# A new order of ScalarE's and VectorE's instructions in a chunked scan and at the start of a gated MLP, in a fused kernel of three layers

## The chip, the cores and the metric

One core of one Trainium2 chip. The metric is the time of one execution on the device in microseconds (us), the median of several runs. A NeuronCore has five engines with in-order instruction streams that meet through semaphores: TensorE (PE, matmuls into PSUM), VectorE (DVE), ScalarE (ACT), GpSimd (POOL) and SyncE (SP, which here only starts DMAs).

## The reference

256 tokens of width 1024, with 16 meta tokens in front in the first block, pass through a hybrid mixer (gated causal convolution beside stick-breaking attention), a conv-gated MLP, a layer of two chunked scans, and a block-sparse attention layer. The two parts that the change touches are the MLP

```python
def conv_gated_mlp(xn, w_up_gate, conv_w_ffn, w_down):
    u, g = jnp.split(xn @ w_up_gate, 2, axis=-1)
    u = causal_dwconv(u, conv_w_ffn)               # width 3, one filter per channel
    return (jax.nn.gelu(u) * g) @ w_down           # 2816 hidden channels
```

and the scan layer, here cut to its order of work:

```python
    u = h @ w_in
    z_a, xbc, dt_raw, q_b, k_b, v_b, gate_lr, g_b = split_cols(u, EVEN_SPLITS)
    xbc = silu(causal_depthwise_conv(xbc, conv_w, conv_b))      # width 4
    y_a = ssd_chunked_scan(xs, dt, a, bm, cm, d)                # 16 heads of 64
    y_a = rms_norm(y_a * silu(z_a), ssd_norm_w)
    o_b = gla_chunked(q_b, k_b, v_b, log_decay)                 # 8 heads, chunks of 64
    o_b = rms_norm(o_b, gla_norm_w) * silu(g_b)
    out = concat([y_a, o_b]) @ w_out
```

`gla_chunked` scores each chunk's queries against its keys, carries a state from chunk to chunk (`decay * s + k^T v`), and adds what the queries read from the state. `ssd_chunked_scan` multiplies a matrix of decays with the scores of `bm` and `cm` and applies it to `dt * xs`.

## The kernel before

**Stream of weights.** All matmuls with weights are done in fp32r with weights and inputs split in a high and a low part, three matmuls for a block of 128 x 128 (high with high, high with low, low with high). `tiles_of_stream` lists the output tiles in PE's order. Almost every tile has 8 blocks, which is one chunk of 0.5 MB (the value tiles `ev` of the scan have two chunks). A chunk is loaded to `raw` by SP, its high part is written by ACT (`split_hi`, L549), the low part by DVE (`split_lo`, L1077); each of the three buffers holds 4 chunks. PE waits on `lo_ready` before it reads a chunk (`project`, L1806; L1809 for `ev`; L1834 for tiles done together). ACT may write the high part of a chunk when PE has read the chunk four before it. `feed(tile)` is this `split_hi` or `split_lo`, once for each chunk of the tile, and on both engines the calls run four chunks ahead: `feed(("eg", 2))` writes the chunk that comes four behind that of eg2, after PE has finished eg2. SP sends the DMA of a chunk when the low part of the one four before it is written.

**Order.** There is no planner: each engine's order is written out by hand in its block, with `feed` calls between the element-wise work. Where an instruction stands in an engine's order decides what waits behind it.

**Feed-forward start.** PE does fu0, fg0 and fu1 together, then fg1, fu2, fg2, fu3, fg3, fu4 and so on (fu: the conv half, fg: the gate half). For tile i DVE scales u (`ffn_up`, L1326), ACT makes the first tap (L738), DVE adds two (`ffn_conv`, L1333), ACT applies GELU (L743), POOL scales it (`ffn_scale`, L452), DVE multiplies it with PE's gate tile (`ffn_out`, L1341), and ACT and POOL split the product (L747, L458). PE may write a tile's PSUM bank when the tile that had it before has been read: fg3's bank is that of fg1, read by `ffn_out(1)`.

**The scan.** Round p (0 to 3) has the tiles eq, ek, ev of the linear attention (GLA; query, key, value of a pair of heads) and, for u = 2p and 2p+1, ez (gate of the state-space part, SSD), eg (gate of GLA) and ex (input of SSD, for u+2). Between the tiles PE does small matmuls:

- `turn_x(u)` (L2068) transposes silu(conv(x)); needs DVE's `ssd_y(u-1)` (L1464), which empties bank 5. `ssd_args(u)` (L1459) on DVE makes of it dt * x.
- `ssd_heads(u)` (L2077) needs `ssd_args(u)` and the decay matrices, which ACT makes (`decays`, L849 and L854) and POOL multiplies with the scores (`ssd_weights`, L479).
- `turn_keys(p)` (L2089) transposes the keys into bank 6, and ACT copies them (`take_keys(p)`, L870). It needs `gla_norm(p-1)` on DVE (its two reads of bank 6, L1497), which needs `gla_rms(p-1)` on ACT (L901, L903, behind a load of the activation table).
- `gla_scores(p)` (L2098) needs the copied keys and POOL's products of queries and keys with the exponentials that ACT makes in `gla_exps(p)` (13 instructions, L888 and L889). DVE masks the scores (L1479).
- `gla_kv(p)` (L2110) makes the chunks' k^T v, DVE's `gla_states(p)` (L1486, L1489) runs them through the recurrence, and `gla_out(p)` (L2120, L2123), which stands between the tiles ek and ev of the next round, needs the result.
- ACT copies ev out of PSUM in `take_values(p)` (L864).

`conv_in` (L1380) takes an ex, eb or ec tile out of PSUM, `tap` (ACT, L778) makes the first of the four taps, `conv_rest` (DVE, L1388) the other three, `z_full` (L1397) and `half_tanh` (ACT, L803) make silu of it or of a gate. `gate_y` (L1469) multiplies SSD's output with its gate, `ssd_high`/`ssd_low` and `gla_high`/`gla_low` split the results for the output projection. `decay_sums(1)` (L1413, L1417) makes the cumulated decays of rounds 2 and 3.

Of the kernel before, what the change touches and what calls it, by code (L numbers as in the profile page):

```python
# [158 lines left out]
def build(nc, xT, params, weights, masks, gate_w2, out, scratch):  # L159
    with ExitStack() as ctx:  # L160
# [362 lines left out]
        def _(act):  # L523
# [27 lines left out]
            def feed(tile):  # L551
                for _ in chunk_of(tile):
                    split_hi()
# [324 lines left out]
            def gla_exps(p):  # L878

                k = p % 2  # L880
                act.wait_ge(S("gla_bias"), p // 2 + 1)
                need(act, "gla_qk", p)
                need(act, "sc_ready", p - 1)
                need(act, "st_ready", p - 1)
                for n, (dst, scale) in enumerate(((kb[:, k, :], 1.0 / 16), (ka[:, k, :], 1.0 / 16), (em, -1.0 / 16))):
                    for c in range(4):
                        w_ = slice(64 * c, 64 * c + 64)
                        a.step(A(dst[:, w_], gcs[:, p, w_], ACT.Exp, scale=scale, bias=decay_cols[:, n, p, c:c + 1]))  # L888
                a.sig(A(eg[:, k, :], gcs[:, p, :], ACT.Exp, scale=-1.0 / 16), "gla_exp")  # L889

            def gla_squares(p):
                act.wait_ge(S("gla_o"), p + 1)
                a.sig(A(osq, bank(6), ACT.Square), "gla_sq")
# [36 lines left out]
            for p in range(1, 4):  # L930
                u = 2 * p
                feed(("ek", p))
                if p == 1:
                    gla_exps(1)
                    take_values(1)
                    feed(("ev", 1))
                    half_tanh(("ex", 3), xs[:, 3, :])
                    gla_squares(0)
                    half_tanh(("ez", 1), zs[:, 1, :])
                    act.wait_ge(S("xsilu"), 6)  # L940
                    half_tanh(("eg", 1), gs[:, 1, :])
                    ssd_high(0)
                    gla_rms(0)
                    feed(("ez", 2))
                    decays(3)
                    ssd_high(1)
                    half_tanh(("ez", 2), zs[:, 0, :])
                else:
                    gla_squares(p - 1)
                    gla_exps(p)  # L950
                    feed(("ev", p))
                    take_values(p)
                    gla_rms(p - 1)
                    feed(("ez", u))
                    half_tanh(("ez", u), zs[:, 0, :])
                    decays(u + 1)
                feed(("eg", u))
                half_tanh(("eg", u), gs[:, u % 4, :])
                gla_high(p - 1)
                if p > 1:  # L960
                    take_keys(p)
                if p < 3:
                    feed(("ex", u + 2))
                ssd_high(u)
                if p < 3:
                    tap(("ex", u + 2), u + 2, xs[:, u + 2, :])
                feed(("ez", u + 1))
                if p == 1:
                    take_keys(1)
                if p < 3:  # L970
                    half_tanh(("ex", u + 2), xs[:, u + 2, :])
                half_tanh(("ez", u + 1), zs[:, 1, :])
                if p < 3:
                    decays(u + 2)
                feed(("eg", u + 1))
                half_tanh(("eg", u + 1), gs[:, (u + 1) % 4, :])
                if p < 3:
                    feed(("ex", u + 3))
                ssd_high(u + 1)
                if p < 3:  # L980
                    tap(("ex", u + 3), u + 3, xs[:, u + 3, :])
                    feed(("eq", p + 1))
                    half_tanh(("ex", u + 3), xs[:, u + 3, :])
# [79 lines left out]
        def _(dve):  # L1063
# [279 lines left out]
            ffn_up(0)  # L1343
            ffn_up(1)
            ffn_conv(0)
            feed(("fu", 1))
            ffn_conv(1)
            ffn_out(0)
            feed(("fg", 1))
            ffn_out(1)  # L1350
# [219 lines left out]
            for p in range(1, 4):  # L1570
                u = 2 * p
                take_queries(p)
                if p == 1:
                    take_keys(1)
                    gate_both(0)
                    feed(("eq", 1))
                    conv_rest(("ex", 3), 3, xs[:, 3, :])
                    ssd_y(2)
                    feed(("ek", 1))
                    z_full(("ex", 3), xs[:, 3, :], name="xsilu")  # L1580
                    gate_both(1)
                    feed(("ev", 1))
                    z_half(("ez", 2), zs[:, 0, :])
                    ssd_args(3)
                    gla_norm(0)
                    feed(("ez", 2))
                    ssd_low(0)
                    ssd_low(1)
                else:
                    feed(("eq", p))  # L1590
                    z_full(("ex", u + 1), xs[:, u + 1, :], name="xsilu")
                    ssd_args(u)
                    take_keys(p)
                    feed(("ek", p))
                    feed(("ev", p))
                    ssd_y(u)
                    z_half(("ez", u), zs[:, 0, :])
                    gla_norm(p - 1)
                    feed(("ez", u))
                    ssd_args(u + 1)  # L1600
                z_half(("eg", u), gs[:, u % 4, :])
                feed(("eg", u))
                z_full(("ez", u), zs[:, 0, :])
                gate_y(u)
                z_full(("eg", u), gs[:, u % 4, :])
                gla_low(p - 1)
                if p < 3:
                    conv_in(("ex", u + 2))
                    feed(("ex", u + 2))
                    conv_rest(("ex", u + 2), u + 2, xs[:, u + 2, :])  # L1610
                z_half(("ez", u + 1), zs[:, 1, :])
                feed(("ez", u + 1))
                ssd_low(u)
                if p < 3:
                    z_full(("ex", u + 2), xs[:, u + 2, :], name="xsilu")
                z_half(("eg", u + 1), gs[:, (u + 1) % 4, :])
                ssd_y(u + 1)
                gla_scores(p)
                feed(("eg", u + 1))
                z_full(("ez", u + 1), zs[:, 1, :])  # L1620
                gate_y(u + 1)
                z_full(("eg", u + 1), gs[:, (u + 1) % 4, :])
                ssd_low(u + 1)
                if p == 1:
                    decay_sums(1)
                if p < 3:
                    conv_in(("ex", u + 3))
                gla_states(p)
                if p < 3:
                    feed(("ex", u + 3))  # L1630
                    conv_rest(("ex", u + 3), u + 3, xs[:, u + 3, :])
# [727 lines left out]
```

## Time and profile before

| | |
|---|---|
| median of 3 runs | 846.91 us (846.84 to 847.1) |
| the profiled execution: own time | 846.78 us |
| its span | 844.9 us |
| busy: PE, DVE, ACT, POOL | 830.4, 622.5, 504.9, 120.2 us |
| feed-forward start | 315 to 327 us of the span |
| the scan's rounds 1 to 3 | about 550 to 665 us |
| granted TensorE clock, mean over the span | 0.998 of full speed |

A view of the profile lists, for each instruction or run of equal instructions, its start in us from the span's start, its duration, engine, line, operation and operands, and in brackets how long the engine was idle before it and which instruction ended that. Matmuls are pipelined: in a steady stream they start every 0.12 us and are each shown 0.28 us long, so their starts tell the pace. The chain of waits is what ended last, followed back step by step.

### The profile page before, as it was taken

To read this page: it belongs to the slowest core of one execution; us is meant where nothing else is said; L and a number is where in the kernel's file an instruction comes from. 1 tells how busy PE (TensorE), PEld (TensorE's weight loads), DVE (VectorE), ACT (ScalarE), POOL (GpSimd) and SP (SyncE) were. 2 spreads that over 40 slices of the span, in tenths; PEclk is the share of its full clock that TensorE was granted. 3 is DMA by queue.
4 is the path that set the end of the run, shared out by engine and by line. 5 is a ranking of instruction groups with operands and counts; after the bars stand their busy time and mean duration, and the time that the engine had idled before them with its cause. 6 is when DMAs were issued, how large, how long until landed. Compare 5 with 4: busy or idle time off the path is not lost.

```text
span 844.9 us, 16864 instructions
## 1 busy us (share of the span) xinstructions
PE 830.4 (98%) x6770; PEld 799.7 (95%) x6770; DVE 622.5 (74%) x1055; ACT 504.9 (60%) x876; POOL 120.2 (14%) x119
## 2 busy tenths in 40 slices
PE   8999999999999999999999999999999999999997
PEld 7999999999999999999999999998898999888896
DVE  6647888886666688677664488999797696568765
ACT  6346657555454576555554468797868555356655
POOL 1000000000000305433441100042414010000002
PEclk9999999999999999999999999999999999999999
DMA  8744435445555536655666535545444376654431
GB/s 307 254 153 141 154 104 173 128 138 175 187 181 193 173 101 193 196 188 179 195 194 187 192 101 166 176 153 184 149 152 153 114 229 183 191 169 136 125 101 50
DMA packets 39853, 139.81 MB, mean 165 GB/s; under 512 B 4432, under 2 KB 5088, under 8 KB 39648
## 3 DMA queue, kind: packets, MB, share of 16 engines
q1 hardware_dynamic: 37728, 135.22, 50.1%
q10 hardware_dynamic: 2048, 3.51, 1.3%
q8 instruction: 54, 0.88, 0.5%
q14 instruction: 23, 0.19, 0.1%
HBM read 137.65 MB, written 1.06 MB: 164 GB/s over the span
## 4 chain that ended last, share of the span: by engine, by line
PE 82%; DVE 9%; ACT 5%; issue 1%; DMA 1%; POOL 1%; SPq 0%; DVEq 0%; ACTq 0%; POOLq 0%
PE ps L1806 66%; PE ps L1834 4%; PE ps L1809 4%; DVE weights_lo L1077 3%; ACT weights_hi L549 1%; PE ps L1949 1%; PE ps L1934 1%; DMA raw_weights<-weights_in 1%; PE ps L1963 1%; PE ps L2217 1%; PE ps L2235 1%; DVE arena L1388 1%; PE ps L2225 1%; POOL arena L479 0%; ACT arena L888 0%
## 5 line engine op out<-in xcount | busy, mean ns | idle before, releaser
L1077 DVE TENSOR_TENSOR weights_lo<-raw_weights,weights_hi 128x1024 fp32r<-128x1024 f32 x251 | 311.8, 1247 | 87.1 <-ACT weights_hi L549 86.8
L1806 PE MATMUL ps<-x_hi,weights_hi 128*128 128x256 f32 (+3 forms) x1272 | 367.8, 289 | 1.2 <-DVE weights_lo L1077 0.5
L1806 PE MATMUL ps<-x_lo,weights_hi 128*128 128x256 f32 (+3 forms) x1272 | 358.1, 282 | 0.0
L1806 PE MATMUL ps<-x_hi,weights_lo 128*128 128x256 f32 (+3 forms) x1272 | 357.9, 281 | 0.0
L549 ACT ACTIVATE weights_hi<-raw_weights 128x1024 fp32r<-128x1024 f32 x251 | 263.2, 1053 | 147.6 <-PE ps L1806 61.0
L1806 PEld LDWEIGHTS ps<-x_hi,weights_hi 128*128 128x128 f32 x1272 | 239.2, 188 | 8.7 <-issue 6.0
L1806 PEld LDWEIGHTS ps<-x_lo,weights_hi 128*128 128x128 f32 x1272 | 239.6, 188 | 0.7 <-issue 0.5
L1806 PEld LDWEIGHTS ps<-x_hi,weights_lo 128*128 128x128 f32 x1272 | 239.5, 188 | 0.0
L1806 PE MATMUL ps<-y_hi,weights_hi 128*128 128x256 f32 (+1 forms) x488 | 137.7, 282 | 0.0
L1806 PE MATMUL ps<-y_lo,weights_hi 128*128 128x256 f32 (+1 forms) x488 | 137.4, 282 | 0.0
L1806 PE MATMUL ps<-y_hi,weights_lo 128*128 128x256 f32 (+1 forms) x488 | 137.1, 281 | 0.0
L444 POOL TENSOR_TENSOR arena<-arena 128x256 f32<-128x256 f32 (+1 forms) x24 | 25.9, 1081 | 494.2 <-ACT arena L700 327.7
L1806 PEld LDWEIGHTS ps<-y_hi,weights_hi 128*128 128x128 f32 x488 | 92.0, 189 | 0.3 <-issue 0.2
L1806 PEld LDWEIGHTS ps<-y_lo,weights_hi 128*128 128x128 f32 x488 | 91.9, 188 | 0.3 <-issue 0.2
L1806 PEld LDWEIGHTS ps<-y_hi,weights_lo 128*128 128x128 f32 x488 | 92.0, 189 | 0.0
L452 POOL TENSOR_TENSOR arena<-arena,rinv 128x256 f32<-128x256 f32 x22 | 33.4, 1517 | 81.8 <-ACT arena L743 81.8
L1809 PE MATMUL ps<-weights_hi,x_hi 128*128 128x256 f32 (+1 forms) x96 | 31.0, 323 | 0.6 <-DVE arena L1380 0.6
L1809 PE MATMUL ps<-weights_lo,x_hi 128*128 128x256 f32 (+1 forms) x96 | 30.6, 319 | 0.0
L1809 PE MATMUL ps<-weights_hi,x_lo 128*128 128x256 f32 (+1 forms) x96 | 30.6, 318 | 0.0
L738 ACT ACTIVATE arena<-arena,params 128x256 f32<-128x256 f32 x22 | 11.1, 510 | 28.4 <-DVE arena L1326 28.2
L1326 DVE TENSOR_TENSOR arena<-ps,rinv 128x258 f32<-128x258 f32 x22 | 9.4, 428 | 24.9 <-PE ps L1806 24.2
L1333 DVE SCALAR_TENSOR_TENSOR arena<-arena,params 128x256 f32<-128x256 f32 x44 | 22.2, 505 | 4.2 <-ACT arena L738 1.0
(268 smaller groups left out, 1069.9 us busy)
## 6 DMA issues: line engine op xcount, KB each, us to landing
raw_weights<-weights_in SPq DMA_DIRECT2D x251, 512.0 KB, 3.8
arena<-decay_rows ACTq DMA_DIRECT2D x8, 256.0 KB, 3.9
masks<-masks_in SPq DMA_DIRECT2D x1, 1186.0 KB, 7.1
raw_weights<-weights_in SPq DMA_DIRECT2D x4, 256.0 KB, 6.0
hidden<-xT_in SPq DMA_DIRECT2D x2, 272.0 KB, 6.7
hidden<-xT_in ACTq DMA_DIRECT2D x1, 276.0 KB, 4.0
hidden<-xT_in ACTq DMA_DIRECT2D x1, 272.0 KB, 5.9
gate_w<-gate_w_in ACTq DMA_DIRECT2D x1, 256.0 KB, 3.7
```

Source lines behind the costliest of these rows:

```text
L444: ins = nc.gpsimd.tensor_tensor(sq[:, 0, t0:T], sq[:, 0, t0:T], sq[:, i, t0:T], ALU.add)
L452: g.sig(nc.gpsimd.tensor_tensor(fgl[:, i % 2, :], fgl[:, i % 2, :], rinv[:, META:T], ALU.mult), "gelu_scaled")
L549: a.sig(A(whi[:, s * CW:(s + 1) * CW], raw[:, (c % RAW) * CW:(c % RAW + 1) * CW], ACT.Copy), "hi_ready")
L738: a.sig(A(fcv[:, i % 2, :], fu[:, i % 2, 0:L], ACT.Copy, scale=pcol("conv_ffn", i)), "tap_ready")
L1077: d.sig(TT(wlo[:, s * CW:(s + 1) * CW], raw[:, (c % RAW) * CW:(c % RAW + 1) * CW], whi[:, s * CW:(s + 1) * CW].bitcast(F32), ALU.subtract) ...
L1326: d.sig(TT(fu[:, i % 2, :], r, rinv[:, TA:T], ALU.mult), "u_ready")
L1333: ins = STT(out=c_, in0=u[:, j:L + j], scalar=pcol("conv_ffn", FT * j + i), in1=c_, op0=ALU.mult, op1=ALU.add)
L1388: ins = STT(out=dst, in0=scr2[:, n % 2, j:L + j], scalar=pcol("even_conv", 10 * j + ct), in1=dst, op0=ALU.mult, op1=ALU.add)
L1806: ins = mm(bank(BANK_OF[no])[:, 0:b - a], wt, x_[:, kt, a:b], start=s0, stop=s1)
L1809: ins = mm(bank(BANK_OF[no + o])[0:t1 - t0, 0:step * P], x_[:, kt, t0:t1], wt, start=s0, stop=s1)
L1834: ins = mm(bank(BANK_OF[no])[:, 0:b - a], w_[:, at:at + P], x_[:, kt, a:b], start=kt == 0 and n == 0 and len(passes) == 2, stop=kt == KT - ...
L1934: ins = mm(bank(4 + e)[:, c0:c0 + T - t0], keysT[rows, p, k0:k0 + P], qpair[rows, p % 2, t0:T], start=n == 0, stop=n == 2, skip_group_chec ...
```

## The change

In the order of hunks:

1. ACT, rounds 2 and 3: `feed(("ev", p))` comes ahead of `gla_exps(p)`.
2. ACT, round 1: `take_keys(1)` comes right behind `feed(("eg", 2))`, ahead of the tanh of eg2; before it stood behind `feed(("ez", 3))`.
3. DVE, feed-forward start: `ffn_conv(1)` comes ahead of `feed(("fu", 1))`.
4. DVE, rounds 2 and 3: `ssd_args(u)` comes ahead of `feed(("eq", p))` and of the silu of ex.
5. DVE, round 1: `gla_states(1)` and `conv_in(("ex", 5))` come right behind `feed(("eg", 3))`; before they stood behind `decay_sums(1)`.

No instruction is added or removed; SP, POOL and PE keep their order.

```diff
--- before.py
+++ after.py
@@ -947,14 +947,16 @@
                     half_tanh(("ez", 2), zs[:, 0, :])
                 else:
                     gla_squares(p - 1)
+                    feed(("ev", p))
                     gla_exps(p)
-                    feed(("ev", p))
                     take_values(p)
                     gla_rms(p - 1)
                     feed(("ez", u))
                     half_tanh(("ez", u), zs[:, 0, :])
                     decays(u + 1)
                 feed(("eg", u))
+                if p == 1:
+                    take_keys(1)
                 half_tanh(("eg", u), gs[:, u % 4, :])
                 gla_high(p - 1)
                 if p > 1:
@@ -965,8 +967,6 @@
                 if p < 3:
                     tap(("ex", u + 2), u + 2, xs[:, u + 2, :])
                 feed(("ez", u + 1))
-                if p == 1:
-                    take_keys(1)
                 if p < 3:
                     half_tanh(("ex", u + 2), xs[:, u + 2, :])
                 half_tanh(("ez", u + 1), zs[:, 1, :])
@@ -1343,8 +1343,8 @@
             ffn_up(0)
             ffn_up(1)
             ffn_conv(0)
+            ffn_conv(1)
             feed(("fu", 1))
-            ffn_conv(1)
             ffn_out(0)
             feed(("fg", 1))
             ffn_out(1)
@@ -1587,9 +1587,9 @@
                     ssd_low(0)
                     ssd_low(1)
                 else:
+                    ssd_args(u)
                     feed(("eq", p))
                     z_full(("ex", u + 1), xs[:, u + 1, :], name="xsilu")
-                    ssd_args(u)
                     take_keys(p)
                     feed(("ek", p))
                     feed(("ev", p))
@@ -1617,15 +1617,19 @@
                 ssd_y(u + 1)
                 gla_scores(p)
                 feed(("eg", u + 1))
+                if p == 1:
+                    gla_states(1)
+                    conv_in(("ex", 5))
                 z_full(("ez", u + 1), zs[:, 1, :])
                 gate_y(u + 1)
                 z_full(("eg", u + 1), gs[:, (u + 1) % 4, :])
                 ssd_low(u + 1)
                 if p == 1:
                     decay_sums(1)
-                if p < 3:
-                    conv_in(("ex", u + 3))
-                gla_states(p)
+                else:
+                    if p < 3:
+                        conv_in(("ex", u + 3))
+                    gla_states(p)
                 if p < 3:
                     feed(("ex", u + 3))
                     conv_rest(("ex", u + 3), u + 3, xs[:, u + 3, :])
```

## Rows read from the trace of the kernel before

**Rows 1.** Timeline of TensorE, feed-forward start (start us, us, engine line op operands xcount [idle before <-releaser])

```profile
320.09 0.29 PE L1806 MATMUL ps<-x_hi,weights_hi 128*128 128x258 f32 x1
...
322.83 0.28 PE L1806 MATMUL ps<-x_hi,weights_lo 128*128 128x258 f32 x1
323.45 0.39 PE L1806 MATMUL ps<-x_hi,weights_hi 128*128 128x256 f32 x1 [0.34 <-DVE arena L1341]
...
326.86 0.36 PE L1806 MATMUL ps<-x_hi,weights_hi 128*128 128x258 f32 x1 [0.32 <-DVE weights_lo L1077]
```

**Rows 2.** Timeline of TensorE in the scan: three of its waits

```profile
581.28 1.10 PE L2098 MATMUL ps<-arena 128*128 128x256 f32 x4 [1.49 <-ACT arena L870]
...
593.21 1.05 PE L2120 MATMUL ps<-arena 128*128 128x128 f32 x7 [1.33 <-DVE arena L1489]
...
605.90 0.41 PE L2068 MATMUL ps<-masks,arena 128*128 128x128 f32 x2 [0.49 <-DVE arena L1464]
```

**Rows 3.** Timeline of ScalarE in the scan, rounds 2 and 3

```profile
597.71 2.97 ACT L888 ACTIVATE arena<-arena,decay_columns 128x64 f32<-128x64 f32 x12
...
631.56 0.42 ACT L803 ACTIVATE arena<-arena 128x256 f32<-128x256 f32 x1 [2.17 <-DVE arena L1388]
...
633.30 2.97 ACT L888 ACTIVATE arena<-arena,decay_columns 128x64 f32<-128x64 f32 x12
...
636.48 2.00 ACT L549 ACTIVATE weights_hi<-raw_weights 128x1024 fp32r<-128x1024 f32 x2
638.37 0.82 ACT L864 ACTIVATE arena<-ps,rinv_by_token 128x256 f32<-128x256 f32 x2
```

**Rows 4.** Timeline of VectorE in the scan

```profile
586.33 1.94 DVE L1077 TENSOR_TENSOR weights_lo<-raw_weights,weights_hi 128x1024 fp32r<-128x1024 f32 x1 [0.17 <-ACT weights_hi L549]
...
592.43 0.73 DVE L1489 SCALAR_TENSOR_TENSOR arena<-arena,ps 128x128 f32<-128x128 f32 x2
593.07 1.22 DVE L1077 TENSOR_TENSOR weights_lo<-raw_weights,weights_hi 128x1024 fp32r<-128x1024 f32 x1
...
606.30 0.88 DVE L1497 SCALAR_TENSOR_TENSOR arena<-ps,params,arena 128x256 f32<-128x256 f32 x2
...
612.14 1.95 DVE L1077 TENSOR_TENSOR weights_lo<-raw_weights,weights_hi 128x1024 fp32r<-128x1024 f32 x1 [1.20 <-ACT weights_hi L549]
...
628.03 0.73 DVE L1489 SCALAR_TENSOR_TENSOR arena<-arena,ps 128x128 f32<-128x128 f32 x2
```

**Rows 5.** Timeline of TensorE in the scan, rounds 2 and 3

```profile
608.98 0.38 PE L2089 MATMUL ps<-masks,arena 128*128 128x128 f32 x2
...
629.00 1.05 PE L2120 MATMUL ps<-arena 128*128 128x128 f32 x8
...
636.34 0.88 PE L2077 MATMUL ps<-arena 128*64 128x256 f32 x8
...
647.70 1.78 PE L2077 MATMUL ps<-arena 128*64 128x256 f32 x8
```

**Rows 6.** Chain of waits, 622 to 656 us (start us, us, what)

```profile
647.57 1.01 POOL arena L479
...
648.62 0.86 PE ps L2077 x4
```

**Rows 7.** Timeline of VectorE, feed-forward start

```profile
316.84 1.01 DVE L1333 SCALAR_TENSOR_TENSOR arena<-arena,params 128x256 f32<-128x256 f32 x2 [0.39 <-ACT arena L738]
318.19 1.23 DVE L1077 TENSOR_TENSOR weights_lo<-raw_weights,weights_hi 128x1024 fp32r<-128x1024 f32 x1 [0.34 <-ACT weights_hi L549]
319.52 1.29 DVE L1333 SCALAR_TENSOR_TENSOR arena<-arena,params 128x256 f32<-128x256 f32 x2
```

**Rows 8.** Timeline of GpSimd, feed-forward start

```profile
318.54 1.47 POOL L452 TENSOR_TENSOR arena<-arena,rinv 128x256 f32<-128x256 f32 x1 [21.58 <-ACT arena L743]
...
323.01 0.73 POOL L458 TENSOR_TENSOR y_lo<-arena,y_hi 128x256 fp32r<-128x256 f32 x1
```

**Rows 9.** Weight DMAs of L424 issued from 585 to 640 us

```profile
DMA to landing us min/median/max: 3.4/3.6/5.0
```

## Prediction

> **What bounds the kernel now.** I read the list of TensorE's waits first, then the timelines of all engines around each wait, then the chain of waits from 560 to 660 us. TensorE (PE) is busy nearly all the time, so a change can win only where PE waits, and lose only where it makes PE wait. It waits in the two places that the diff touches. In the feed-forward start the tile fg3 begins at 323.45 instead of 0.12 behind the matmul of 322.83, and fu4 begins at 326.86 [rows 1]. In the scan it waits 1.49 us for the turned keys of round 1 (`klt`, L870 on ScalarE), 1.33 us for the states of the same round (`gla_states(1)`, L1489 on VectorE), and about 0.5 us for `ssd_y(4)` [rows 2]. The profile's figure for a wait is too small by 0.16: at 323.45 it says 0.34, while the starts are 0.62 apart where 0.12 is the rhythm, so 0.50 is lost.
>
> These waits are one half of the picture. The other half is that ScalarE (ACT) and VectorE (DVE) pass work back and forth through every round without slack: ACT waits for the DVE's conv taps (L1388) at 631.56 [rows 3], DVE waits for ACT's `split_hi` at 612.14 [rows 4], and so on; round 2 and 3 of ACT's exponentials are 35.6 us apart (597.71, 633.30) [rows 3]. PE isn't in that loop. It is tied to it again late in round 3: `ssd_heads(7)` begins at 647.70 and takes 1.78 us [rows 5], because GpSimd (POOL) finishes its second product at 648.58 and the last four matmuls start at 648.62 [rows 6]. Whatever PE has won earlier is handed back at such a place unless the loop is shorter too.
>
> **Feed-forward start.** `ffn_conv(1)` moves ahead of `feed(("fu", 1))` on DVE. Its two instructions cost 1.01 alone, as `ffn_conv(0)` does at 316.84 [rows 7]. So they end at 317.85 + 0.07 + 1.01 = 318.93, 1.9 us earlier than now (319.52 + 1.29 = 320.81). GELU(1) on ACT and its scaling on POOL then no longer hold `ffn_out(1)`: the wait at 323.45 (0.50) goes. DVE is 0.7 earlier at `feed(("fu", 2))`, and the wait at 326.86 (0.32 + 0.16) goes too. Both first matmuls also have the next one 0.23 and 0.19 behind instead of 0.12. Together 1.1 at most.
>
> The cost is what was moved past: `feed(("fu", 1))` writes the low half of the weights of fu3 (feeds run four chunks ahead). It runs 318.19 to 319.42 now [rows 7] and PE wants it at 320.09 [rows 1]. Behind the conv it starts at 318.9, so even alone it ends at 320.1. It isn't alone. POOL asks for its scaling at 318.54: beside DVE's split that took 1.47, a like one by itself takes 0.73, and DVE's pair of 319.52 took 1.29 instead of 1.01 [rows 7, 8]. So each turn costs DVE 0.28, and two splits in a row beside POOL cost more. With 0.28 the split ends at 320.4 to 320.5, PE waits 0.4 and gets 0.1 more from the restart: net gain 1.1 - 0.5 = 0.6. With a full POOL instruction in between (0.73 and restart) it ends near 321.1 and the gain is gone (-0.1). Bounds 1.1 and -0.1; I take 0.5, since the 0.28 is the nearest row.
>
> The Trainium skill (SBUF — State Buffer, Who interferes with whom) says that GpSimd and a VectorE instruction with two SBUF inputs exclude each other, one blocking fully. The rows agree in kind. By that rule the split would wait for the whole rest of the POOL instruction, and this stage would give 0.2 instead of 0.5.
>
> **Scan, round 1.** `take_keys(1)` moves from behind `feed(("ez", 3))` to behind `feed(("eg", 2))`. There ACT idles before its next tanh, and the 0.36 us copy hides; the turned keys are long there. PE's `gla_scores(1)` starts without the wait: 1.49 + 0.16 = 1.65 [rows 2]. `gla_states(1)` and `conv_in(("ex", 5))` move ahead of four gate instructions and `decay_sums(1)` on DVE. The states end at 593.16 now [rows 4]; moved, they follow the split of 586.33, which ends at 588.27, and are done by about 589.3. `gla_out(1)` then has no wait: 1.33 + 0.16 = 1.5 [rows 2]. PE reaches the value tile ev2 about 3.2 us earlier. DVE's sum of work is the same, so `feed(("ex", 5))` still begins near 593.07 and ends near 594.29 [rows 4], and PE, which wants it now at 594.4, just isn't held.
>
> **Round 2.** `feed(("ev", 2))` goes ahead of `gla_exps(2)` on ACT. Each of its two instructions waits for PE to have read a chunk of ev2, and all of ACT's later work is queued behind. Today ev2 ends 7.34 us behind `gla_out` (629.00 to 636.34 [rows 5]), that is at 593.21 + 7.4 = 600.6; moved 3.2 earlier, at 597.4. ACT wants the second feed at 597.71 + 0.95 = 598.66, so it doesn't wait. `ssd_y(4)` comes some 3 us earlier with the feeds, and `ssd_args(4)` 1.5 earlier, which PE needs by then. But ACT's sum is unchanged, so `gla_rms(1)` ends when it did, `gla_norm(1)` still runs at 606.30 and its two reads end at 607.18 [rows 4]. PE can't turn the keys before that (bank 6): 607.2 against 608.98 now [rows 5], so at most 1.7 of the 3.2 is left. Then `gla_states(2)`, which is not moved, still ends at 628.03 + 0.73 = 628.76 [rows 4], while `gla_out(2)` runs at 629.00. Of the gain 0.1 to 0.2 is left at ev3.
>
> **Round 3.** The same swap now meets a PE that isn't early. ACT is free for the feeds at 633.30. The first ends at 634.25, (638.37 - 636.48) / 2 = 0.95 each [rows 3]. The second waits until ev3 is complete, 636.34 less 0.1 [rows 5], so ACT stands for 2.0 us with `gla_exps(3)` (636.48 - 633.30 = 3.18) behind it. `take_values(3)` comes at 636.3 + 0.95 + 3.18 = 640.4 instead of 638.37: 2.1 late. Behind it, with nothing in between that has slack, stand `gla_rms(2)`, two table loads, `decays(7)`, POOL's products and `ssd_heads(7)`, at which PE waits already [rows 5, 6]. So PE loses the whole 2.1 there, and whatever `turn_x(7)` gains before is lost with it. After that all engines are shifted alike.
>
> **Sum.** 846.78 us (the profiled execution's own time, of which its span is 844.9) - 0.5 + 2.1 = 848.4. The median of the runs is 0.13 above the profiled one: 848.5. The scan's gains of 3.2 are in no sum, as they end at waits for the loop.
>
> **The rivals.** *Faster: PE's waits count in full.* If ACT and DVE had slack that I don't see, the removed waits add up: 1.1 + 1.65 + 1.5 + some 1.2 for the wait of 605.90 and one like it a round later = 5.5, that is 841.4; with the feed-forward's lock 842. For it speaks only that the waits are on the chain of waits; against it 606.30, 628.76 and 648.62. The Trainium skill (Perfetto Trace Analysis, Optimization Strategies) advises just this, to optimise the engines that block the matmul engine while it waits. By its rule the time would be this rival's. Chance 0.13.
>
> *Same: ACT's stand in round 3 doesn't reach PE*, or PE is early enough at ev3 after all (`gla_states(2)` 2 us earlier). Then the scan gives 0 to -0.2 and the sum is 846.91 - 0.5 (to 1.1) = 845.8 to 846.4. Against it is the 1.78 us at 647.70. Chance 0.14.
>
> *Slower: ACT stands in round 2 as well.* The place is the second feed of ev2. It needs PE at ev2 at least 2.0 us earlier than now (600.6 - 598.66), of the 3.2 worked out; and it needs its raw weights, whose DMA can start at 594.3 and lands 3.4 to 5.0 later (median 3.6) [rows 9], 597.7 to 599.3 against 598.66. From there each microsecond lengthens the loop one to one, and round 3 comes on top. Price 0.3 to 2.0: 848.8 to 850.5. Chance 0.13.
>
> **How the numbers follow.** The forecast as worked out has 0.60, with its own range 847.4 to 849.4 (the feed-forward from 1.1 gained to 0.1 lost, ACT's stand 1.8 to 2.3). About 0.2% (1.7 us) is what a measurement of this kernel can tell from no change, so "slower" begins at 848.6, just above the forecast: of the 0.60 I give 0.32 to "same" and 0.28 to "slower". With the rivals: faster 0.13, same 0.32 + 0.14 = 0.46, slower 0.28 + 0.13 = 0.41. The range leaves out the fast rival (0.13) and the far end of the slow one (0.07): 845.8 to 849.9.
>
> **What would show it.** Right: no wait before the matmuls of L2098 and of the first L2120 at about 590; new waits of PE at the key turns L2089 (about 1.6) and at L2120 in round 2 (1.5, for L1489); ACT idle 2 us before a `split_hi` (L549), waiting for PE's value tile, some 34 us after the exponentials of round 2; `ssd_heads(7)` of 3 us and more; in the feed-forward a wait at fu3 instead of those at fg3 and fu4. Wrong: an ACT without that wait, a `gla_norm(1)` or `gla_states(2)` earlier than the shift of the stage before them, or a PE that waits at fu3 for more than 1 us. The forecast falls altogether if the period of 35.6 us between the rounds on ACT becomes shorter.

## The result, and the profile after

| | before | after |
|---|---|---|
| median (lowest to highest of 16) | 846.91 us (846.83 to 847.22) | 848.75 us (848.42 to 849.09) |
| the profiled execution: own time, span | 846.78, 844.9 us | 848.86, 847.0 us |
| ratio after to before, 95% interval | | 1.0021, 1.0014 to 1.0029 |

The change makes the kernel 1.84 us slower, 0.22%. No instruction was added or removed, and the page of the kernel after shows the same work; only the span is longer.

```profile
span 847.0 us, 16864 instructions
## 1 busy us (share of the span) xinstructions
PE 830.8 (98%) x6770; PEld 799.8 (94%) x6770; DVE 621.3 (73%) x1055; ACT 505.4 (60%) x876; POOL 116.0 (14%) x119
```

PE of after has the same line numbers as before plus 4 (L1810 for L1806, L2124 for L2120 and so on). First its waits, summed by line (engine line waited for: us in total, times, longest us):

```profile
PE ps L2093 <- DVE arena L1497: 2.6, 2, 1.6
PE ps L2081 <- POOL arena L479: 1.6, 2, 1.4
PE ps L2124 <- DVE arena L1489: 1.3, 1, 1.3
...
PE ps L1810 <- DVE weights_lo L1077: 0.7, 2, 0.6
...
PE ps L2072 <- DVE arena L1464: 0.4, 1, 0.4
```

The waits of [rows 2] have gone, for the turned keys and for the states of round 1. In their place stand the key turn (L2093), in rounds 2 and 3, the states of round 2 (L2124) and POOL's products in round 3 (L2081). Where they lie is in PE's timeline of the scan:

```profile
579.56 0.81 PE L2102 MATMUL ps<-arena 128*128 128x256 f32 x3
...
589.92 1.05 PE L2124 MATMUL ps<-arena 128*128 128x128 f32 x8
...
602.42 0.41 PE L2072 MATMUL ps<-masks,arena 128*128 128x128 f32 x2 [0.40 <-DVE arena L1464]
...
607.21 0.41 PE L2093 MATMUL ps<-masks,arena 128*128 128x128 f32 x2 [1.57 <-DVE arena L1497]
...
628.69 1.16 PE L2124 MATMUL ps<-arena 128*128 128x128 f32 x8 [1.25 <-DVE arena L1489]
...
649.59 0.83 PE L2081 MATMUL ps<-arena 128*64 128x256 f32 x4 [1.41 <-POOL arena L479]
650.65 0.86 PE L2081 MATMUL ps<-arena 128*64 128x256 f32 x4 [0.22 <-POOL arena L479]
```

`gla_out(1)` runs at 589.92 instead of 593.21, 3.3 us early [rows 2]. At the key turn 1.77 us of it are left (607.21 against 608.98), at `gla_out(2)` 0.31 (628.69 against 629.00), and `ssd_heads(7)` is late: 649.59 instead of 647.70 [rows 5]. What went wrong between 629 and 648 is on ScalarE:

```profile
597.60 1.99 ACT L549 ACTIVATE weights_hi<-raw_weights 128x1024 fp32r<-128x1024 f32 x2
599.49 1.29 ACT L888 ACTIVATE arena<-arena,decay_columns 128x64 f32<-128x64 f32 x5
...
631.43 0.42 ACT L803 ACTIVATE arena<-arena 128x256 f32<-128x256 f32 x1 [2.18 <-DVE arena L1388]
...
633.43 1.06 ACT L549 ACTIVATE weights_hi<-raw_weights 128x1024 fp32r<-128x1024 f32 x1
636.27 1.06 ACT L549 ACTIVATE weights_hi<-raw_weights 128x1024 fp32r<-128x1024 f32 x1 [1.77 <-PE ps L1813]
637.23 2.97 ACT L888 ACTIVATE arena<-arena,decay_columns 128x64 f32<-128x64 f32 x12
...
640.41 0.82 ACT L864 ACTIVATE arena<-ps,rinv_by_token 128x256 f32<-128x256 f32 x2
```

In round 2 the two feeds of ev2 follow each other without a wait (597.60, 1.99 for both). In round 3 the second feed of ev3 waits 1.77 us until PE has read the value tile, with the exponentials behind it. `take_values(3)` starts at 640.41 instead of 638.37 [rows 3], 2.04 late. POOL's products begin at 648.44 in the trace of after (646.41 before), and the first tile behind `ssd_heads(7)` begins 2.0 us late (651.44 against 649.42). The shift lasts to the end: PE's last small matmuls start at 840.48, 838.41 before.

The feed-forward start in three timelines, of PE, DVE and POOL:

```profile
320.81 0.36 PE L1810 MATMUL ps<-x_hi,weights_hi 128*128 128x258 f32 x1 [0.58 <-DVE weights_lo L1077]
...
323.74 0.28 PE L1810 MATMUL ps<-x_hi,weights_hi 128*128 128x256 f32 x1
...
326.58 0.29 PE L1810 MATMUL ps<-x_hi,weights_hi 128*128 128x258 f32 x1
```

```profile
316.86 2.12 DVE L1333 SCALAR_TENSOR_TENSOR arena<-arena,params 128x256 f32<-128x256 f32 x4 [0.41 <-ACT arena L738]
318.90 1.77 DVE L1077 TENSOR_TENSOR weights_lo<-raw_weights,weights_hi 128x1024 fp32r<-128x1024 f32 x1
```

```profile
318.56 1.02 POOL L452 TENSOR_TENSOR arena<-arena,rinv 128x256 f32<-128x256 f32 x1 [21.62 <-ACT arena L743]
```

The waits at fg3 and fu4 have gone, and fu3 has a new one of 0.58. fu4 starts 0.28 early (326.58 against 326.86 [rows 1]); behind its first matmul, which no longer loses time to a restart, the lead is 0.35.

### The profile page after: what moved, and what is told of

The parts are those of the page before. It is cut to its first block, busy times and chain, and to the rows that moved or that the text cites. A ratio compares the mean times of both kernels' runs of the same rounds, so it can differ in the third digit from the quotient of the medians.

```text
span 847.0 us, 16864 instructions
## 1 busy us (share of the span) xinstructions
PE 830.8 (98%) x6770; PEld 799.8 (94%) x6770; DVE 621.3 (73%) x1055; ACT 505.4 (60%) x876; POOL 116.0 (14%) x119
## 4 chain that ended last, share of the span: by engine, by line
PE 81%; DVE 9%; ACT 6%; issue 2%; DMA 1%; POOL 1%; SPq 0%; DVEq 0%; ACTq 0%; POOLq 0%
PE ps L1810 65%; PE ps L1838 4%; PE ps L1813 4%; DVE weights_lo L1077 3%; ACT weights_hi L549 1%; PE ps L1953 1%; PE ps L1938 1%; DVE arena L1388 1%; DMA raw_weights<-weights_in 1%; PE ps L1967 1%; PE ps L2221 1%; PE ps L2239 1%; ACT arena L888 1%; ACT arena L849 1%; PE ps L2229 1%
## 5 line engine op out<-in xcount | busy, mean ns | idle before, releaser
L1810 PE MATMUL ps<-x_hi,weights_hi 128*128 128x256 f32 (+3 forms) x1272 | 367.5, 289 | 1.2 <-DVE weights_lo L1077 0.7
L1810 PE MATMUL ps<-x_lo,weights_hi 128*128 128x256 f32 (+3 forms) x1272 | 358.6, 282 | 0.0
L1810 PE MATMUL ps<-x_hi,weights_lo 128*128 128x256 f32 (+3 forms) x1272 | 357.8, 281 | 0.0
L1810 PEld LDWEIGHTS ps<-x_hi,weights_hi 128*128 128x128 f32 x1272 | 239.3, 188 | 8.5 <-issue 6.0
L1810 PEld LDWEIGHTS ps<-x_lo,weights_hi 128*128 128x128 f32 x1272 | 239.4, 188 | 0.7 <-issue 0.5
L1810 PEld LDWEIGHTS ps<-x_hi,weights_lo 128*128 128x128 f32 x1272 | 239.8, 188 | 0.0
L1810 PE MATMUL ps<-y_hi,weights_hi 128*128 128x256 f32 (+1 forms) x488 | 137.6, 282 | 0.0
L1810 PE MATMUL ps<-y_lo,weights_hi 128*128 128x256 f32 (+1 forms) x488 | 137.4, 282 | 0.0
L1810 PE MATMUL ps<-y_hi,weights_lo 128*128 128x256 f32 (+1 forms) x488 | 137.1, 281 | 0.0
L1810 PEld LDWEIGHTS ps<-y_hi,weights_hi 128*128 128x128 f32 x488 | 92.0, 189 | 0.3 <-issue 0.2
L1810 PEld LDWEIGHTS ps<-y_lo,weights_hi 128*128 128x128 f32 x488 | 91.9, 188 | 0.3 <-issue 0.2
L1810 PEld LDWEIGHTS ps<-y_hi,weights_lo 128*128 128x128 f32 x488 | 92.0, 189 | 0.0
```

What stands on the lines that cost most here:

```text
L1810: ins = mm(bank(BANK_OF[no])[:, 0:b - a], wt, x_[:, kt, a:b], start=s0, stop=s1)
```

## The experiments

Each kernel was timed beside the kernel before on the same chip, in eleven executions (e3 eight, e8 ten). The median of before lay between 846.78 and 846.98 in these jobs, and the single times of a kernel lie about 0.25 us to either side of their median, so a difference of 0.2 us between medians is at the edge of what is seen; the 95% intervals are about 0.09% to either side. Besides the changed kernel itself only e3, e4 and e12 have an interval that leaves out 1. For e6 and e8 the single times speak more clearly: none of theirs is above 846.32, and none of the 33 of before in the same job is below 846.47. What e1 and e2 win can't be told from nothing by the interval. Hunk 4 and the round 2 half of hunk 1 were not tried by themselves; e2 has both.

| kernel | median, us | before, us | ratio, 95% |
|---|---|---|---|
| e1 conv order only | 846.67 | 846.88 | 0.9997 (0.9988 to 1.0006) |
| e2 after, round 3's feeds back | 846.62 | 846.88 | 0.9997 (0.9988 to 1.0006) |
| e3 round 3's feeds only | 849.08 | 846.88 | 1.0027 (1.0016 to 1.0037) |
| e4 round 1's moves only | 847.82 | 846.88 | 1.001 (1.0002 to 1.0019) |
| e5 after, states of round 2 early | 847.27 | 846.85 | 1.0004 (0.9995 to 1.0013) |
| e6 last decays early | 846.01 | 846.85 | 0.9992 (0.9983 to 1.0) |
| e7 e2, states and decays early | 846.09 | 846.98 | 0.9994 (0.9985 to 1.0003) |
| e8 e1 without POOL's first scaling | 846.05 | 846.85 | 0.9991 (0.9982 to 1.0) |
| e9 e4 with matmuls in the gap | 846.85 | 846.85 | 1.0 (0.9991 to 1.0009) |
| e10 e5 with decays early | 846.40 | 846.98 | 0.9994 (0.9985 to 1.0003) |
| e11 e7 with matmuls in the gap | 847.01 | 846.78 | 1.0002 (0.9993 to 1.0011) |
| e12 e6 with e1's order | 845.85 | 846.78 | 0.9988 (0.9979 to 0.9997) |

### Where the loss is: the feeds of round 3

A stand is a stretch in which an engine does nothing but wait. The theory is that ACT's stand at the second feed of ev3 is the whole loss. e2 undoes that swap in the kernel after, e3 makes it alone in the kernel before.

```diff
# e2, against after
                     gla_squares(p - 1)
-                    feed(("ev", p))
+                    if p == 2:
+                        feed(("ev", p))
                     gla_exps(p)
+                    if p == 3:
+                        feed(("ev", p))
```

> The kernel after, with round 3's feeds of the value tile back behind the exponentials (round 2 keeps them ahead). Theory (ScalarE's stand of 1.8 us before the second feed of round 3 is the whole loss): 848.75 - 2.05 = 846.7 us, GpSimd's products of the last pair of heads at 646.3 as before, no wait of ScalarE for PE's value tile. Rival (the loss comes from TensorE's waits at the key turns, 1.57 us in round 2 and 1.01 in round 3, or from the scan's round 1): the wait of round 2 stays, so at least 848.2 us.

```diff
# e3, against before
                     gla_squares(p - 1)
+                    if p == 3:
+                        feed(("ev", p))
                     gla_exps(p)
-                    feed(("ev", p))
+                    if p == 2:
+                        feed(("ev", p))
```

> The kernel before with one edit: in round 3 alone the feeds of the value tile ahead of the exponentials. Theory: ScalarE stands until the value tile is done (636.4), 2.1 us, and all of it reaches the end: 846.91 + 2.1 = 849.0 us. Rival (the loss needs the other edits too, for instance TensorE's earlier arrival): at most 847.4 us.

e2 gave 846.62, e3 849.08: one swap carries the loss, +2.20 alone and 2.13 less when it is undone in after. In e3's timelines of ACT and of PE the same two waits stand as in after:

```profile
636.78 1.06 ACT L549 ACTIVATE weights_hi<-raw_weights 128x1024 fp32r<-128x1024 f32 x1 [1.79 <-DVE weights_lo L1080]
```

```profile
650.10 0.84 PE L2080 MATMUL ps<-arena 128*64 128x256 f32 x4 [1.43 <-POOL arena L479]
```

The releaser of e3's wait is written as DVE's split here and as PE in after; the instruction waits for several semaphores, and the one that came last by the profile is named. e2 settles that the wait comes from the feed's place: with the feeds behind the exponentials ACT has no such wait, and `take_values(3)` starts at 638.21. That it is a wait for PE shows in the times: the last matmul of ev3 ends at 636.18 in after, 636.70 in e3 and 634.38 in e5 (below), and the second feed starts 0.08 to 0.09 us later in each (636.27, 636.78, 634.46).

e2 shows a second thing. Its PE waits between 575 and 660 us are

```profile
PE ps L2096 <- DVE arena L1500: 1.6, 1, 1.6
PE ps L2127 <- DVE arena L1492: 1.2, 1, 1.2
PE ps L2075 <- DVE arena L1467: 0.9, 2, 0.5
```

3.7 us together. Before has in the same stretch

```profile
PE ps L2098 <- ACT arena L870: 1.5, 1, 1.5
PE ps L2120 <- DVE arena L1489: 1.3, 1, 1.3
PE ps L2068 <- DVE arena L1464: 0.9, 2, 0.5
```

which is 3.7 us too. Two waits were removed, others of the same sum appeared, and the time moved by 0.26 us, of which the conv order (e1) is 0.21. Letting PE come earlier moved its waits for the loop of ACT and DVE along the scan and didn't make them fewer. The advice of the Trainium skill (Perfetto Trace Analysis, Optimization Strategies) that the prediction took as a rival, to optimise the engines that block the matmul engine, brought nothing at the two waits of round 1; at `ssd_heads(7)` (e6 below) it brought 0.84 us.

### The feed-forward start

```diff
# e1, against before
             ffn_conv(0)
+            ffn_conv(1)
             feed(("fu", 1))
-            ffn_conv(1)
```

> The kernel before with one edit: the second feed-forward conv ahead of the feed (hunk 3). Theory: the scan isn't touched, so the time is that of before less what the feed-forward start gives in the trace of after, 0.1 to 0.36 us: 846.6 to 846.8, and PE waits 0.6 us at fu3 (start near 320.8) with no wait at fg3 and fu4. Rival (the 0.36 us that PE was ahead at 330 us in the kernel after is not worn away by 490 us, its loss there was chance): 846.5 or less. Rival (the conv order itself is the loss): above 847.5.

It gave 846.67, 0.21 less than before where the prediction took 0.5. The split took 1.76 us in it, as in after, and PE waited 0.59. e8 takes away what the split shares its time with: POOL's first scaling.

```diff
# e8, against e1
-            ffn_scale(0)
+            pool.wait_ge(S("gelu_ready"), 1)
+            g.sig(nc.gpsimd.memset(aw[:, 1, 0:1], 0.0), "gelu_scaled")
             ffn_scale(1)
```

> The kernel with only the second feed-forward conv moved, but GpSimd leaves out the scaling of the first GELU tile (its product with the inverse rms is missing, one of 22 tiles of the hidden layer) and sets one word in its place. Theory (VectorE's weight split behind the two convs ended late, at 320.67, because GpSimd's scaling stood in its way): the split ends at 320.1, TensorE's wait at fu3 shrinks from 0.6 to at most 0.2 us, and the time is 0.4 to 0.5 us under that of the conv order alone: 846.2 us. Rival (the split is late by its place in the order alone): the wait stays 0.6 us and the time 846.7.

It gave 846.05, 0.80 less than before and 0.59 more than e1's gain. DVE's timeline has

```profile
318.95 1.22 DVE L1078 TENSOR_TENSOR weights_lo<-raw_weights,weights_hi 128x1024 fp32r<-128x1024 f32 x1
```

and fu3 starts at 320.31 with a wait of 0.02. So POOL's instruction costs the split 0.55 us (1.77 less 1.22), not the 0.28 that the prediction took from DVE's conv pair. When the split starts in after (318.90), POOL's instruction has 0.68 us to go (318.56 + 1.02 = 319.58). The Trainium skill (SBUF — State Buffer, Who interferes with whom) speaks of an exclusive lock; 0.55 of 0.68 comes close to it, and the 0.2 that the prediction gave as the result by that rule is what e1 measured.

### Round 1 alone, and the clock

```diff
# e4, against before (with it take_keys(1) leaves its place behind feed(("ez", 3)))
                 feed(("eg", u))
+                if p == 1:
+                    take_keys(1)
...
                 feed(("eg", u + 1))
+                if p == 1:
+                    gla_states(1)
+                    conv_in(("ex", 5))
...
-                if p < 3:
-                    conv_in(("ex", u + 3))
-                gla_states(p)
+                else:
+                    if p < 3:
+                        conv_in(("ex", u + 3))
+                    gla_states(p)
```

> The kernel before with the edits of round 1 alone (keys taken earlier on ScalarE; states and conv_in(ex5) earlier on VectorE). Theory: TensorE is 3.2 us early at the value tile of round 2 and hands all of it back at waits for VectorE (key turn, ssd_y, states of round 2), since the loop between ScalarE and VectorE keeps its period of 35.6 us: 846.7 to 847.0 us. Rival (TensorE's waits count in full): 846.9 - 3.2 = 843.7 us.

It gave 847.82: neither theory, but 0.94 slower. PE waits 0.87 us at `ssd_heads(4)` (598.39, for `ssd_args(4)`), then once more, for longer than at any place in after, and behind that its rhythm is slower:

```profile
605.98 0.41 PE L2072 MATMUL ps<-masks,arena 128*128 128x128 f32 x2 [2.82 <-DVE arena L1464]
...
606.83 0.42 PE L1810 MATMUL ps<-x_lo,weights_hi 128*128 128x256 f32 x1
607.04 0.41 PE L1810 MATMUL ps<-x_hi,weights_lo 128*128 128x256 f32 x1
607.26 0.41 PE L1810 MATMUL ps<-x_hi,weights_hi 128*128 128x256 f32 x1
```

The starts are 0.21 apart instead of 0.12. The same stretches in windows (us, PE, PEld, DVE, ACT, POOL busy, granted clock, DMA share, GB/s):

```profile
604.00:606.00 2.00, 0.02 (x1) 0.05 (x1) 1.90 (x3) 1.96 (x3) 1.92 (x2) 1.00 0.57 135
606.00:608.00 2.00, 2.00 (x12) 2.00 (x13) 1.95 (x5) 1.98 (x3) 1.70 (x4) 0.63 0.72 227
608.00:610.00 2.00, 2.00 (x11) 2.00 (x11) 1.93 (x2) 1.99 (x5) 0.51 (x1) 0.52 0.40 162
610.00:612.00 2.00, 2.00 (x20) 2.00 (x19) 0.85 (x2) 2.00 (x5) 1.02 (x1) 1.00 0.56 160
```

The granted clock is down at its lower level, 1.2 GHz; in the timeline the slower pace lasts from 606.61 to 609.82, 3.2 us. The eight blocks of the tile take 4.6 us (606.14 to 610.74) instead of 3.1, and PE, which was at the pace of the loop when it waited, is now behind it: the key turn starts at 610.58 instead of 608.98, and the tile behind `ssd_heads(7)` at 650.52 instead of 649.42. In before and in after the clock stands at 1.00 there. Ten of e4's eleven times are 847.41 to 848.07 at a mean clock of 0.996 or 0.997; the eleventh is 846.89 at 0.999, the time of before. Only one execution, of 847.90, has a trace; that the clock fell in the other nine is read from their times and mean clocks.

e9 puts eight matmuls of ones into the gap, into a bank that is free, and is otherwise e4.

```diff
# e9, against e4
+                if p == 2:
+                    for _ in range(8):
+                        mm(bank(SSB)[:, 0:L], ones, mask("ones"), start=True, stop=True)
                 if p:
                     turn_x(u + 1)
```

> The kernel with the edits of round 1 alone, and eight matmuls of ones (128 x 256, results unused) in TensorE's order between ez4 and turn_x(5), where it stood for 2.8 us and where the granted clock then fell to half for 3.2 us. Theory (of the 0.9 us that the round-1 edits alone lose, all is the fall of the clock behind that one long stand): with the stand filled the clock stays at full speed and the time is 846.9 us (846.7 to 847.1). Rival (the loss is an ordinary wait, or the waits of the loop have grown): 847.8 us or more with the clock at full speed.

It gave 846.85, all eleven between 846.71 and 847.21, and the clock stayed:

```profile
606.00:608.00 2.00, 2.00 (x18) 1.90 (x17) 1.95 (x5) 1.98 (x3) 1.78 (x3) 1.00 0.68 225
608.00:610.00 2.00, 2.00 (x19) 2.00 (x19) 1.90 (x3) 1.99 (x6) 0.39 (x1) 1.00 0.25 98
```

The filling took a little more than the gap (`turn_x(5)` at 606.31, 605.98 in e4), and still the time is that of before. So the moves of round 1 bring nothing by themselves, and the one long stand cost 0.9 us through the clock. In after, where the feeds of ev2 and `ssd_args(4)` come earlier as well, PE waits 0.40, 1.57 and 1.25 us instead; which of the two moves splits the stand wasn't tried.

### Could round 3's swap be made harmless?

The "same" rival said that PE only has to be early enough at ev3. e5 gives it `gla_states(2)` early.

```diff
# e5, against after
-                if p == 1:
-                    gla_states(1)
-                    conv_in(("ex", 5))
+                if p < 3:
+                    gla_states(p)
+                    conv_in(("ex", u + 3))
```

> The kernel after, with the states of round 2 and conv_in(ex7) moved ahead on VectorE as round 1 has them. Theory (the loss is ScalarE's stand until the value tile of round 3 is done, and its length is how late TensorE is there): TensorE's wait of 1.25 us at the output matmuls of round 2 goes, the value tile ends 1.5 us earlier (634.7 instead of 636.2), ScalarE's stand shrinks from 1.8 to about 0.3 us, and the time falls as much: 848.75 - 1.5 = 847.2 us. Rival (the swap costs what it costs wherever TensorE is, for instance by its order on VectorE or GpSimd): 848.7 us, unchanged.

847.27. `gla_out(2)` has no wait (626.97), and in ACT's timeline the second feed comes at

```profile
634.46 1.06 ACT L549 ACTIVATE weights_hi<-raw_weights 128x1024 fp32r<-128x1024 f32 x1 [0.52 <-issue]
```

instead of 636.27: the stand is 0.5 instead of 1.8, and ACT comes to it 0.54 earlier, so `take_values(3)` starts 1.80 earlier than in after (638.61). The kernel is 1.48 faster by the medians, 1.85 between the profiled executions. So the swap's cost goes with how late PE is at ev3; the 0.37 between the two differences is how far the two profiled executions lie from their medians.

### The place where PE is tied to the loop

If `ssd_heads(7)` is where all is handed back, then letting its inputs come earlier should win where the whole change did not. e6 is the kernel before with one move on ACT.

```diff
# e6, against before
                     gla_rms(p - 1)
+                    if p == 3:
+                        decays(7)
                     feed(("ez", u))
                     half_tanh(("ez", u), zs[:, 0, :])
-                    decays(u + 1)
+                    if p == 2:
+                        decays(5)
```

> The kernel before with one edit: in round 3 ScalarE makes the decays of the last pair of heads right behind gla_rms(2), ahead of a feed, a table load and a tanh. Theory (TensorE's end of the scan hangs on ScalarE's decays and GpSimd's products at 648.6): the products are done before 647 and TensorE's wait of 0.9 us inside ssd_heads(7) and its restart go: 846.9 - 1.0 = 845.9 us. Rival (something else holds TensorE there or right behind): 846.9 us.

846.01, 0.84 less than before; the tile behind `ssd_heads(7)` begins 0.81 earlier (648.61). In the timelines of POOL and PE the products end at 647.24 instead of 648.6, and the matmuls take 0.88 instead of the 1.78 of [rows 5]:

```profile
644.27 2.97 POOL L479 TENSOR_TENSOR arena<-arena 128x384 f32<-128x384 f32 x2
```

```profile
647.80 0.88 PE L2080 MATMUL ps<-arena 128*64 128x256 f32 x8
```

e7 joins e2, the early states of e5 and these early decays; e10 adds the early decays to e5.

> The kernel after with round 3's feeds back behind the exponentials, the states of round 2 early, and the last decays early on ScalarE. Theory (each step as measured alone): from 846.62 us for the feeds put back, less 0.9 for the decays; the 1.4 us that the early states bring TensorE are lost again at turn_x(7), where it then stands some 2 us for ssd_y(6), whose feeds now come late again: 845.7 us. Rival (early states count in full): 844.3 us. Rival (the stand at turn_x(7) is long enough that the granted clock falls): 846.5 us or more, with a stretch at half clock behind 641 us.

> The kernel after with the states of round 2 early and the last decays early, the feeds of round 3 staying ahead of the exponentials. Theory: from 847.27 us, TensorE's stands of 1.43 and 0.22 us before and inside ssd_heads(7) go but for about 0.3 (GpSimd's products end near 647), while its stand of 1.0 us at the key turn of round 3 stays: 845.6 us. Rival (another wait takes their place right behind): 846.5 us or more.

e7 gave 846.09, but its eleven times are in two groups: six of 845.78 to 846.09 at a mean clock of 0.998 or 0.999, and five of 847.12 to 847.43 at 0.996 or 0.997. The profiled execution is of the upper group. PE stands 1.95 us at `turn_x(7)`, and then the windows say

```profile
641.35 0.41 PE L2076 MATMUL ps<-masks,arena 128*128 128x128 f32 x2 [1.95 <-DVE arena L1470]
```

```profile
640.00:642.00 2.00, 0.65 (x6) 0.68 (x7) 1.88 (x4) 1.96 (x4) 1.92 (x2) 1.00 0.77 260
642.00:644.00 2.00, 2.00 (x13) 2.00 (x13) 1.97 (x4) 2.00 (x7) 1.68 (x3) 0.64 0.63 219
644.00:646.00 2.00, 2.00 (x11) 2.00 (x11) 1.27 (x2) 1.98 (x2) 1.82 (x2) 0.51 0.14 53
```

e10 gave 846.40 at a full clock: its stand of 0.5 at the second feed is still there, the decays begin at 642.35, and PE waits 0.89 at `ssd_heads(7)` for DVE's `ssd_args(7)`. The 845.6 expected of it took no account of that engine.

e11 is e7 with eight matmuls of ones ahead of `turn_x(7)` (as in e9, for `p == 3`).

> The kernel of the run that joins the three moves (last-round feeds back, round 2's states early, last decays early), and ahead of the turn of x(7) in the last round eight matmuls of ones into a bank that is free. They fill part of the 1.95 us in which TensorE stood there. The eleven times of that kernel fall into two groups, 845.78 to 846.09 at a mean clock of 0.998 or 0.999 and 847.12 to 847.43 at 0.996 or 0.997. Theory (the upper group is the clock's fall to its lower level behind that stand, and nothing else): one group only, 845.7 to 846.2, median 845.9, and the clock 1.00 in the profile from 640 to 648. Rival (the two groups have another cause, a transfer or a table load): both groups stay.

847.01, all eleven between 846.80 and 847.07. The two groups have become one and the clock is 1.00 from 640 to 648, as the clock theory says; the level is 1.1 us above the 845.9 that it gave. PE's timeline shows why:

```profile
639.02 3.62 PE L2165 MATMUL ps<-masks 128*128 128x256 f32 x16
642.47 0.38 PE L2076 MATMUL ps<-masks,arena 128*128 128x128 f32 x2
```

The filling took more than the gap: `turn_x(7)` runs at 642.47 instead of 641.35, 1.12 late, and 845.9 + 1.1 is the time measured. So e11 shows one group without the fall, but not the time regained, as e9 does for e4. That fewer matmuls would hold the clock at 845.9 wasn't tried.

e12 joins e6 and e1, two places with nothing in common.

> The kernel before with the last decays early (846.01 alone, 0.84 less than before) and the second conv of the feed-forward ahead of the feed (846.67 alone, 0.21 less). The two places are 320 us apart with no wait between them. Theory (gains that no later wait takes back add up): 846.85 - 0.84 - 0.21 = 845.8. Rival (the feed-forward's gain is worn away by the scan, where VectorE and ScalarE set the pace and TensorE waits for them): 846.0.

845.85, 0.93 less than before in the same job: the two gains add up to within 0.12. Theory and rival are only 0.2 apart, and the time is between them, so e12 doesn't decide whether some of the feed-forward's gain is worn away. It is the fastest version here, 2.9 us below the changed kernel, with an interval that just excludes no change.

## Why the prediction was right, and where not

The forecast was 848.5 in a range of 845.8 to 849.9; measured 848.75. The range of the forecast by itself, given as 847.4 to 849.4, comes out of its stated parts as 847.6 to 849.3; nothing hangs on that. The time fell on the slower side of the bound of 0.2% by a hair (0.22%), where "same" had been given a little more than "slower". By its steps:

- **ACT's stand in round 3.** Worked out 2.0 to 2.1, from 633.30, 636.34 and the 3.18 us of exponentials. `take_values(3)` was 2.04 late, e3 alone cost 2.20, e2 took 2.13 off. Right, with mechanism and size.
- **All that is won before is handed back.** Worked out: key turn of round 2 at 607.2 with about 1.6 of wait (607.21, 1.57), 1.5 for L1489 (1.25), 0.1 to 0.2 left at ev3 (0.2), new wait at L2077 and `ssd_heads(7)` of 3 us and more (with its waits of 1.41 and 0.22 it takes from 648.2 to 651.5, 3.3). A wait of 1.01 at the key turn of round 3 (L2093, two in the list of waits) the prediction hadn't named; it is part of the same lateness, as e3 has it and e2 doesn't. e2 is the proof: PE's new waits cost nothing. The period of the loop, 35.6 us before [rows 3], can't be read between the exponentials of round 2 and 3 after the swap, but at the tanh of ex ahead of them: 595.85 to 631.43 in after, 595.96 to 631.56 before, 35.58 and 35.60. The loop didn't become shorter.
- **The round 2 swap is free.** ACT's two feeds took 1.99 us with no wait, as said; the "slower" rival (a stand there too) didn't come true. PE reached ev2 3.4 us early, 3.2 worked out.
- **Feed-forward start: the mis-sized term.** 0.5 was taken; e1 measured 0.21. By the traces it is somewhat more: at the tile that begins at 332.62 in before, the traces with the new order (e8 aside) are 0.22 to 0.51 early (mean 0.38), the four others with the old one 0.12 early to 0.09 late; the intervals don't tell 0.2 from 0.4. The mechanism was right (waits at fg3 and fu4 gone, one at fu3 instead), but the term "each turn costs DVE 0.28" was too small: the row was of a pair of conv instructions beside POOL, and the split lost 0.55 in e1 and after (e8). Nearest in shape would have been the split itself beside POOL. The prediction's own sum with 0.28 gave 0.6, of which it took 0.5. With 0.2 instead of 0.5 the sum is 848.8.
- **What was missing.** The prediction counted a wait of PE at its length. It had no term for the clock, and that none was needed for this change is luck: its other moves cut the stand in pieces, which the prediction didn't ask for. Half of the change alone (e4) would have been forecast at 846.9 and is 847.8.

## What to carry to other kernels

Before a wait of the busiest engine is counted as a gain, look for the next place at which that engine is tied to the loop of the others, and ask whether their loop gets shorter; here of 3.4 us won by the start of round 2's value tile 0.3 were left at 629 us, while one move at the last such place (e6) brought 0.84. A refill of a ring buffer is a wait for the reader of that buffer: moved ahead of other work in an in-order queue it is free while the reader is early (round 2) and costs its whole stand when it isn't (round 3), so each round is to be worked out by itself. And several short stands of TensorE need not cost the same as one long one: look at the granted clock behind the long one.

## What the runs showed of the hardware

- Behind a stand of 2.82 us (e4) and of 1.95 us (e7) the granted clock went to its lower level for some 3 us each, 0.52 and 0.51 in a window of 2 us, which cost 0.9 us (e4 over before, where e9 costs nothing) and 1.4 us (e7, between its groups). By times and mean clocks it fell in ten of eleven executions of e4 and in five of eleven of e7, with one trace of each; it didn't fall in the scan in the other twelve profiled executions, whose stands there are of 1.57 us (after) or shorter. What decides it in a given execution is open. The Trainium skill (TensorE: Matmul & The Clock Gate, What's actually happening) gives the two levels as 1.2 and 2.4 GHz; the shares of 0.52 and 1.00 in e4's windows agree with it.
- A split of 128 x 1024 on VectorE took 1.22 us alone (e8) and 1.77 beside a GpSimd instruction that started 0.34 us before it (after).
- The matmul rhythm differs a little from one profiled execution to the next: between the tile that begins at 332.62 in before and the one at 423.61, with no wait between them, the other traces take between 0.01 us less and 0.21 us more than before, nearly all of them either 0.0 or 0.2. A lead of some tenths read from one trace is therefore weak evidence; the medians decide.
